# A two-layer block stack on one core: full-size matrix products in a gated recurrence, hooks moved ahead of waits, and a reordered first load

## The reference, cut to what matters

```python
def hgrn2_mixer(uq, uf, ui, ug, lb, norm_w):          # H = 8 heads of 128, chunks of L = 64, nc = 4
    logf = heads(jnp.log(lb + (1.0 - lb) * jax.nn.sigmoid(uf32)))
    k = heads((1.0 - lb) * jax.nn.sigmoid(-uf32))
    q = heads(jax.nn.silu(uq.astype(F32)))
    v = heads(ui.astype(F32))
    gc = jnp.cumsum(logf, axis=3)
    g_ref = gc[:, :, :, L // 2:L // 2 + 1, :]
    att = jnp.einsum('bhcld,bhcsd->bhcls', q * jnp.exp(gc - g_ref), k * jnp.exp(g_ref - gc))
    att = jnp.where(causal, att, 0.0)
    o = jnp.einsum('bhcls,bhcse->bhcle', att, v)
    s_local = jnp.einsum('bhcsd,bhcse->bhcde', k * jnp.exp(gc[..., -1:, :] - gc), v)
    # s_prev: the states before each chunk, state = chunk_decay * state + s_local
    o = o + jnp.einsum('bhcld,cbhde->bhcle', q * jnp.exp(gc), s_prev)
    o = head_rms_norm(o, norm_w, H) * jax.nn.silu(ug.astype(F32))
```

## Time and profile before

| | us |
|---|---|
| median of 3 runs | 3732.5 (3721.35 to 3736.83) |
| profiled execution, its own time | 3727.36 |
| its span | 3725.5 |
| PE busy | 3012.9 (81%) |
| DVE busy | 2462.2 (66%) |
| first stage | ends at about 21.5 |
| stages F to H | about 1264 to 1410 |

### The profile page before, as it was taken

The page is one execution under the profiler, slowest core; times in us unless marked ns, Lnnn a source line. Parts: engine busy times, 40 slices in busy tenths (PEclk is TensorE's granted clock), DMA queues, the critical chain, the costliest instruction groups (busy, mean ns, idle before and its releaser), DMA issues. The chain is left out here.

```text
span 3725.5 us, 45704 instructions
## 1 busy us (share of the span) xinstructions
PE 3012.9 (81%) x17536; PEld 2351.4 (63%) x17536; DVE 2462.2 (66%) x4571; ACT 774.6 (21%) x1919; POOL 624.9 (17%) x516
## 2 busy tenths in 40 slices
PE   7687796778786898677777779977877999975898
PEld 7576783333332588533433339976767999975798
DVE  4342467777776675777777758754446878765686
ACT  1313221222222232222221220012223001013300
POOL 0000003445444100244444520000000000000000
PEclk9899897888889899788998889978988999987999
DMA  6252358999999533799999966633203666640464
GB/s 192 69 168 66 115 167 342 412 411 415 415 409 421 215 127 117 286 413 417 414 406 410 420 274 181 193 96 102 80 28 115 171 190 166 187 150 6 119 182 153
DMA packets 468969, 858.87 MB, mean 231 GB/s; under 512 B 18704, under 2 KB 398352, under 8 KB 402320
## 3 DMA queue, kind: packets, MB, share of 16 engines
q0 software_dynamic: 73728, 536.90, 35.0%
q1 hardware_dynamic: 394880, 317.49, 28.1%
q10 hardware_dynamic: 144, 1.55, 0.1%
HBM read 848.55 MB, written 7.34 MB: 230 GB/s over the span
## 5 line engine op out<-in xcount | busy, mean ns | idle before, releaser
L2124 PE MATMUL banks<-arena,arena 128*128 128x512 f32 x1792 | 940.3, 684 | 342.5 <-ACT arena L2180 342.0
L2124 PEld LDWEIGHTS banks<-arena,arena 128*128 128x128 f32 x1792 | 382.9, 220 | 882.7 <-issue 454.5
L2084 POOL DMA_INDIRECT arena<-in_peer_uv,arena x512 | 624.7, 1220 | 1571.1 <-DVE arena L2266 877.2
L2289 DVE CUSTOM_DVE_ANT_0 arena<-arena,normed 128x1024 f32<-128x1024 f32 x512 | 626.1, 1223 | 262.7 <-DMA arena<-in_peer_uv,arena 260.7
L352 DVE TENSOR_TENSOR weight_ring_part<-weight_ring,weight_high_parts 128x2048 fp32r<-128x2048 f32 (+2 forms) x244 | 539.9, 2213 | 8.4
L2782 PE MATMUL banks<-normed_columns_part,weight_high_parts 128*128 128x256 f32 x1408 | 403.9, 287 | 10.8 <-PEq L300 9.0
L2783 PE MATMUL banks<-normed_part,weight_high_parts 128*128 128x256 f32 x1408 | 402.2, 286 | 0.0
L2784 PE MATMUL banks<-normed_columns_part,weight_ring_part 128*128 128x256 f32 x1408 | 402.0, 286 | 0.0
L349 DVE CAST weight_high_parts<-weight_ring 128x2048 fp32r<-128x2048 f32 (+2 forms) x244 | 288.3, 1182 | 143.4 <-PE banks L657 80.9
L655 PE MATMUL banks<-weight_high_parts,arena_part 128*128 128x256 f32 x1216 | 344.6, 283 | 41.8 <-PEq L300 28.9
L656 PE MATMUL banks<-weight_ring_part,arena_part 128*128 128x256 f32 x1216 | 342.1, 281 | 0.0
(11 more groups left out here) (499 smaller groups left out, 4358.2 us busy)
## 6 DMA issues: line engine op xcount, KB each, us to landing
weight_ring<-in_ffn_w_gate SPq DMA_DIRECT2D x88, 512.0 KB, 4.0
weight_ring<-in_ffn_w_up SPq DMA_DIRECT2D x88, 512.0 KB, 5.3
weight_ring<-in_ev_w_in SPq DMA_DIRECT2D x33, 1024.0 KB, 5.6
weight_ring<-in_ffn_w_down SPq DMA_DIRECT2D x32, 1024.0 KB, 5.2
weight_ring<-in_od_w_in SPq DMA_DIRECT2D x23, 1024.0 KB, 5.4
weight_ring<-in_xa_wkv SPq DMA_DIRECT2D x16, 1024.0 KB, 5.9
weight_ring<-in_peer_wq SPq DMA_DIRECT2D x16, 1024.0 KB, 5.7
weight_ring<-in_ev_w_out SPq DMA_DIRECT2D x12, 1024.0 KB, 5.6
```

The costliest lines, as they stand in the source:

```text
L2084: pool.indirect_dma_start(out=ring[:, slot(i, s), :], out_offset=None, in_=table, in_offset=bass.IndirectOffsetOnAxis(ap=index[:, i % 2, s ...
L2124: mm = pe.matmul(k.ps[:, 2 * b + half, :], diag[:, n % 2, s, :], v, start=h == 0 and g == 0 and s == 0, stop=h == PEER_HEADS - 1 and g == ...
L2289: dve.tensor_tensor_reduce(out=ring[:, here, 0:D], in0=ring[:, here, 0:D], in1=k.xn[:, b, :], scale=1.0, scalar=0.0, op0=ALU.mult, op1=ALU ...
```

## The change

1. **First stage.** SP issues x, then weight tile 0, then the constants without the identity, the small rows and the other tiles. ACT issues the identity alone, then the feature columns. PE waits for x and the identity only. DVE keeps the low parts of the first two feature chunks, splits tile 0, and then keeps the others. The waits for the other constants and the small rows stand on PE ahead of the first norm's spreading product.
2. **Hooks.** In `columns_out` and `rows_out` the hooks of DVE and ACT are called ahead of the wait for the part or tile instead of behind its work. In F the hook at part m still handles part m-1; the last part's sigmoids and scaling move to the start of stage Q.
3. **Head step.** All products of H take full 128 by 128 shapes: `end_rows` becomes `ends` with one 128-row block for each of three chunks and zeros in the other half, and the weighed queries go to `readers`, with zeros beside each chunk. `give` makes 2 products with att and 3 with the readers; `put` makes 3 over 128 rows. ACT copies the end keys in two instructions, DVE writes the readers in two, and POOL writes the zeros in stage G with four memsets.

```diff
@@ feed(self, sp)
-    def feed(self, sp):
-        while self.issued < min(len(self.plan), self.taken + RING):
+    def feed(self, sp, ahead=RING):
+        while self.issued < min(len(self.plan), self.taken + ahead):
@@ scale_tensor
+        if self.first_norm:
+            pe.wait_ge(self.const_in.sem, 16)
+            pe.wait_ge(self.fetched.sem, 16)
@@ columns_out, DVE
                 for m, (i, j) in enumerate(parts):
+                    if vector_then is not None:
+                        vector_then(dve, m)
                     dve.wait_ge(self.produced.sem, self.produced.start + m + 1)
                     evacuate(dve, m, self.ps[:, m % BANKS, 0:T]).then_inc(self.evacuated.sem, 1)
                     if j == tiles[i] - 1:
                         self.split_next(dve, self.taken + 1)
-                    if vector_then is not None:
-                        vector_then(dve, m)
@@ rows_out, ACT and DVE (pool_first: a hook for POOL)
                     for j in range(len(widths) if on == "scalar" else 0):
+                        if scalar_then is not None:
+                            scalar_then(act, j)
                         for b in range(NB):
                             read(act, j, b)
-                        if scalar_then is not None:
-                            scalar_then(act, j)
...
                 for j in range(len(widths)):
+                    if vector_then is not None:
+                        vector_then(dve, j)
...
                     self.split_next(dve, self.taken + 1)
-                    if vector_then is not None:
-                        vector_then(dve, j)
@@ load_constants
             sp.dma_start(k.x[:, :, :], ...).then_inc(k.x_in.sem, 16)
-            sp.dma_start(k.cols[:, :], k.ins["cols"]).then_inc(k.cols_in.sem, 16)
+            k.feed(sp, ahead=1)
+            sp.dma_start(k.const[:, P:], k.ins["consts"][:, P:]).then_inc(k.const_in.sem, 16)
             sp.dma_start(k.small[:, :], ...).then_inc(k.fetched.sem, 16)
             k.feed(sp)
...
-            act.dma_start(k.const[:, :], k.ins["consts"]).then_inc(k.const_in.sem, 16)
+            act.dma_start(k.c("ident"), k.ins["consts"][:, 0:P]).then_inc(k.ident_in.sem, 16)
+            act.dma_start(k.cols[:, :], k.ins["cols"]).then_inc(k.cols_in.sem, 16)
...
-            k.split_next(dve, 2)
             dve.wait_ge(k.cols_in.sem, 16)
-            dve.wait_ge(k.turned.sem, k.turned.start + D // WIDTH)
             for t in range(D // WIDTH):
+                if t == 1:
+                    k.split_next(dve, 2)
                 k.keep_low(dve, t, gain, high, low)
-            dve.wait_ge(k.fetched.sem, 16)
@@ odd_mixer, stage F
+        if m == H - 1:
+            return None
         act.activation(key[:, m, :], forget[:, m, :], ACT.Sigmoid, scale=-1.0).then_inc(k.gated.sem, 1)
-        return act.activation(forget[:, m, :], forget[:, m, :], ACT.Sigmoid)
+        act.activation(forget[:, m, :], forget[:, m, :], ACT.Sigmoid).then_inc(k.gated.sem, 1)
...
     def gates_behind(dve, m):
         if m:
-            scale_gates(dve, m - 1)
-        if m == H - 1:
-            scale_gates(dve, m)
+            scale_gates(dve, m - 1, 2 + 2 * m)
@@ stage Q (last_gates is its vector_first)
+    def last_gates(dve):
+        scale_gates(dve, H - 1, 2)
     def take_logs(act):
+        last = forget[:, H - 1, :]
+        act.activation(key[:, H - 1, :], last, ACT.Sigmoid, scale=-1.0).then_inc(k.gated.sem, 1)
+        act.activation(last, last, ACT.Sigmoid).then_inc(k.gated.sem, 1)
         for m in range(H):
+            if m == H - 1:
+                act.wait_ge(k.gate_scaled.sem, k.gate_scaled.start + 2)
             act.activation(forget[:, m, :], forget[:, m, :], ACT.Ln).then_inc(k.logged.sem, 1)
@@ stage G
+    def clear(pool):
+        pool.memset(ends[half[1], :, 0::2, :], 0.0).then_inc(k.cleared.sem, 1)
+        ...
+        pool.memset(ends[half[0], :, 1, :], 0.0).then_inc(k.cleared.sem, 1)
+        ...
+        pool.memset(readers[:, :, 0, :], 0.0).then_inc(k.cleared.sem, 1)
+        ...
+        pool.memset(readers[:, :, 3, :], 0.0).then_inc(k.cleared.sem, 1)
@@ stage H, put
                 for c in range(n - 1):
-                    rows = slice(c % 2 * L, (c % 2 + 1) * L)
-                    mm = pe.matmul(input_bank(c), end_rows[rows, h, c // 2, :], vals[rows, c // 2, h * P:(h + 1) * P],
-                                   start=True, stop=True)
+                    mm = pe.matmul(input_bank(c), ends[:, h, c, :], vals[:, c // 2, h * P:(h + 1) * P], start=True, stop=True)
@@ give
-                for c in range(n):
-                    b, rows = c // 2, slice(c % 2 * L, (c % 2 + 1) * L)
-                    mm = pe.matmul(out_bank(h)[rows, b, :], att[rows, h, b, rows], vals[rows, b, h * P:(h + 1) * P],
-                                   start=True, stop=c == 0)
-                    if c:
-                        mm = pe.matmul(out_bank(h)[rows, b, :], q[:, h, c * L:(c + 1) * L], states[:, h, c - 1, :],
-                                       start=False, stop=True)
+                for b in range(NB):
+                    pe.matmul(out_bank(h)[:, b, :], att[:, h, b, :], vals[:, b, h * P:(h + 1) * P], start=True, stop=False)
+                    for c in range(max(2 * b, 1), 2 * b + 2):
+                        mm = pe.matmul(out_bank(h)[:, b, :], reader(h, c), states[:, h, c - 1, :], start=False, stop=c == 2 * b + 1)
@@ keep_ends (ACT)
-                act.activation(end_rows[:, h, :, :], end_bank(h), ACT.Copy).then_inc(k.end_kept.sem, 1)
+                act.activation(ends[half[0], h, 0::2, :], end_bank(h)[half[0]], ACT.Copy).then_inc(k.end_kept.sem, 1)
+                act.activation(ends[half[1], h, 1, :], end_bank(h)[half[1], 0, :], ACT.Copy).then_inc(k.end_kept.sem, 1)
@@ DVE, in place of the product with total at L2731
+            def read_from(h):
+                for at, c0, c1 in ((1, 1, 3), (4, 3, 4)):
+                    t = slice(c0 * L, c1 * L)
+                    dve.tensor_tensor(readers[:, h, at:at + c1 - c0, :].rearrange("p a t -> p (a t)"), q[:, h, t], total[:, h, t],
+                                      ALU.mult).then_inc(k.weighted.sem, 1)
```

More of the change, by code:

```diff
@@ L2449, in odd_mixer @@
     kend = k.take(H, T)
-    end_rows = k.take(H, NB, P)
+    ends = k.take(H, n - 1, P)
+    readers = k.take(H, 5, L)
     att = k.take(H, NB, P)
@@ L2456, in odd_mixer @@
     kg = shifted = forget
+    half = [slice(0, L), slice(L, P)]
     def chunked(ap):
@@ L2546, in odd_mixer, with reader @@
     dump = k.gain_memory[:, 0, :]
+    def reader(h, c):
+        at = (0, 2, 3)[c - 1]
+        return readers[:, h, at:at + 2, :].rearrange("p a t -> p (a t)")
     def att_bank(h):
@@ L2582, in put @@
             def put(h):
-                pe.wait_ge(k.end_kept.sem, k.end_kept.start + h + 1)
+                pe.wait_ge(k.end_kept.sem, k.end_kept.start + 2 * (h + 1))
                 if h:
```

50 lines of the change are left out of this document (32 added, 18 removed).

## The result

| | before | after |
|---|---|---|
| median, us | 3733.93 (13 executions, 3721.35 to 3756.30) | 3714.53 (13 executions, 3702.16 to 3720.13) |
| profiled execution, own time | 3727.36 | 3716.57 |
| its span | 3725.5 | 3714.8 |

The ratio of the executions is 0.9931, interval 0.9914 to 0.9948: some 26 us faster (19 to 32), the medians are 19.4 apart. The forecast was -11. The two profiled executions differ by 10.7 us, and the span of 3714.8 lies 0.3 from the 3714.5 of the sum. So two questions are open: whether the steps inside the sum hold, and where the other 8 to 15 us are that only the timed executions show.

What follows compares the result with a forecast made beforehand. TensorE is busiest at 81%, but the engine ending each touched stage counts. Terms -5.0 + 3.05 + 0.4 - 2.4 - 2.2 - 4.8 = -11.0 took span 3725.5 to 3714.5; forecast median 3721.5, range 3709 to 3731.

Steps and rivals of the forecast that it cites:

- The first stage: First loads: x lands at about 6.5 us and the stage ends at 16.5 instead of 21.5, -5.0 us.
- F: Recurrence stage F: DVE waits for ACT's sigmoids ahead of even scalings, 6.27 us per tile against PE's 5.76, +3.05 us.
- V: Recurrence stage V: ACT's last exponentials move ahead of the evacuations, so the stage ends earlier, -2.4 us.
- G: Recurrence stage G: DVE's last products move ahead and PE's shorter idleness returns some clock, -2.2 us.
- Q: Recurrence stage Q: -0.1 us at its end, +0.5 for a longer low clock after more PE idleness, +0.4 in all.
- the hooks save everywhere: Rival, chance 0.13: F isn't stretched, -1.5 us, and the clock stays up in Q and G; -19.6 us in all, 3712.9.
- x lands no earlier: Rival, chance 0.08: landing is latency, not bytes; the first stage gains only 1.7 us from DVE's order; about -7.5, 3725.
- POOL's zeros hold up DVE, slower: Rival, chance 0.05: POOL's memsets block DVE's splits in stage G; 13.5 us of blocking eats the gain.
- The 3721.5: Whole kernel: the forecast median after the change, the median of before less 11 us, or -0.3%.
- the median of before less 11: Last step of the sum: the profiled execution lies 5 us below the median, so the -11 us is applied to the median.
- The term for H: Head step: full products at 0.27 us cut PE's cycle from 3.63 to 2.98 us over eight heads, -4.8 us.
- Everything else keeps its instructions and moves as a whole: Stages outside the first and the recurrence's five: they only move earlier or later, with no term of their own.

Runs made afterwards that it cites:

- its repair: The changed kernel, with stage F's hook at part m scaling part m-2 and the last two parts scaled in Q: median 3708.07 us, ratio 0.9912 against before.
- The cut kernel's profile: The kernel before, cut off behind the gated recurrence, later stages left out: 1449.56 to 1462.63 us; the profiled execution is one of two at clock 0.880.
- the entry behind 9.31 us of idleness, in the kernel before: The kernel before, cut off behind the gated recurrence, with 130 satisfied waits on PE ahead of the head step: 1451.52 to 1460.03 us.
- the one behind 7.90 us, with the hooks: The kernel before with only the hooks moved, cut off behind the gated recurrence, with 130 satisfied waits ahead of the head step: 1456.34 to 1480.32 us.
- the head step alone: The kernel before with only the full 128 by 128 products of the head step and POOL's zeros: median 3716.15 us, ratio 0.9943.

## Why the prediction was wrong

**What held.** The first stage (-5.3 for -5.0), F (+3.0 for +3.05, by the named mechanism, confirmed by its repair), V (-2.5 for -2.4) and G (-2.0 for -2.2). Q came out at -0.15 for +0.4: the low stretch of the clock at its start is 3.4 us long before and after, though PE idled 3.31 us ahead of it instead of 2.32, and so the 0.5 us for a longer one wasn't paid. The rivals "the hooks save everywhere", "x lands no earlier" and "POOL's zeros hold up DVE, slower" fell; the last one's mechanism exists (2.78 for 1.23) and had the cover that was named. The 3721.5 went by a median of 3732.5 from three executions; the sum on the profile's own span was right to 0.3 us. Part of that is luck: the 1.3 by which the edited stages gained more and the 6.4 of the rwkv stage cancel against the 7.9 lost ahead of F.

**The step that failed** is the last of "The sum": "the median of before less 11". It takes the difference between profile and median as an offset that both kernels share. It isn't: the profiled execution of before lies 10 us below the mean of its executions (3727.4 and 3737.4), that of the change 2.6 above its own (3716.6 and 3714.0). Of 90 executions of before, 40 ran at a mean clock under 0.899, of 53 after the change or with either of its recurrence parts none did. The cut kernel's profile shows one way to such a time: the head step at the low clock from start to end, +18.3 us. The term for H stood on a row at clock 1.00 and had no price for the other case. On the means: 3737.4 - 3731.3 = 6.1 us of before come from the executions under 0.899. The rest, 3731.3 - 3714.0 = 17.3, is near the 12.3 from the edited stages and the 6.4 that the rwkv stage shows.

The rivals didn't hold this case either. Two sentences came near: that PE's idleness ahead of H sets the clock at its start, worth 1.2 us, and that full shapes might cost what tiling saves. What was missed is that a step of partial shapes can stay at the low clock from start to end, which is worth 18 us where it happens.

**"Everything else keeps its instructions and moves as a whole"** is the second miss. Instructions were kept, but their place in PE's stream was not. The rwkv stage, priced at nothing, was 6.4 us shorter, with one stop of PE for instructions instead of two; 62 added waits moved it from 257.2 to 264.2.

**A term mis-sized twice:** H, -5.4 for -4.8. A full product was taken at 0.27, from two of them between transposes and partial products. In a step of full shapes alone it is 0.22, and the cycle of PE 2.45 instead of 2.98. Eight times the further 0.53 would have given 4.2 us more, and 0.6 came. The rest went to PE's waits at the start of the pipeline: the `put` behind the weight split waited 2.11 us where the prediction had a delay of 1.0, and the first iterations waited 0.56 and 0.58 for ACT and DVE. That DVE would not bind in the iterations with a gating held. That the price of one product depends on its neighbours' shapes agrees with the Trainium skill, TensorEngine Tiling (Array Packing), Key Properties, by which a change of the tiling mode drains the TensorE.

**What stays open.** Three things. Why does the entry behind 9.31 us of idleness, in the kernel before, let the clock return under the old shapes, and the one behind 7.90 us, with the hooks, not? Why does the rwkv stage with one stop take 257.2 us in the changed kernel and 260.6 with the head step alone, one record away? And the low head step in the full kernel is inferred from the clocks of its executions: no profile of the full kernel caught one, so how much of the 6.1 us belongs to it isn't shown.

## What to carry to other kernels

Look at the mean granted clock of every execution before carrying a profile's difference over to a median: a step that sits at either clock level in different executions has two prices, and a profile shows one. Where PE works in small or partial products behind a pause, full shapes with zeros may be worth more for the clock than for the products. A stage of very small products can change its length by instructions added or taken out long before it, so compare the lengths of untouched stages too. And in a hook that waits for another engine's round trip, lag by one more part: from F to the next stage it gave 5.7 us here.

## What the runs showed of the hardware

- A long low level in spite of work. In the head step with partial shapes the granted clock stayed at 0.50, 1.2 GHz, for 51.2 and 58.0 us while PE's records followed each other without a gap (4.00 of 4.00 us). The Trainium skill, TensorE: Matmul & The Clock Gate, What's actually happening, says that the throttled state is the default and activity releases it. By that, PE's gapless records should have released it; here they did not, and the measurement decides: busy in the records isn't enough. With the same partial shapes the clock came back in other executions, after 3.4 us and after 10.2 us.
- PE can outrun its instructions. At some 200 products and weight loads per us it stood still for 1.1 to 2.3 us without a wait, beside 16 KB packets on the instruction queue. Two such stops were 255 or 256 records apart, and satisfied waits put ahead moved them by half a record each.
- A DVE cast of 128 by 2048 took 2.78 instead of 1.23 us beside a POOL memset of 1.81. The Trainium skill, SBUF — State Buffer, SBUF: two separate sides, calls the port pair that the two share an exclusive lock. The trace agrees: the cast ends 1.08 us behind the memset (1352.24 and 1351.16), and the next memset, of half the size, takes 1.91.
- A full 128 by 128 product took 0.22 us among its like and 0.27 between partial ones. Of these, the 64 by 128 ones of `put` took 0.21 (its full ones 0.22), and those of `give`, whose shapes alternate, 0.31.
